# Half of an output projection done inside the last head's chunk loop, half a tile at a time

## The reference

```python
y = jnp.concatenate([y_hy, y_ml, y_rg], axis=-1)      # (2048, 1024)
x = x + gate2 * (y @ w_out)                            # output projection and residual
h = rmsnorm(x, norm2_g) * (1 + scale) + shift          # second norm
x = x + gate5 * (jnp.square(jax.nn.relu(h @ w1)) @ w2) # MLP, width 4096
out = rmsnorm(x, final_g)
```

## Time and profile before

| what | value |
|---|---|
| median of 3 runs | 2757.82 us |
| the profiled execution, its own time | 2759.13 us |
| its span in the profile | 2757.3 us |
| PE busy | 2550.4 us, 92% of the span |
| DVE busy | 1710.4 us, 62% |
| ACT busy | 1009.5 us, 37% |
| POOL busy | 456.4 us, 17% |

### The profile page before, as it was taken

One profiled execution on the slowest core, in us unless ns is written; L12 is line 12 of the kernel. 1 busy time (PEld: TensorE's weight loads), 2 busy tenths in 40 slices (PEclk: granted clock), 3 DMA queues, 4 the chain that ended last, 5 costly groups with the idle time before them and its releaser, 6 DMA issues.

```text
span 2757.3 us, 37657 instructions
## 1 busy us (share of the span) xinstructions
PE 2550.4 (92%) x14948; PEld 1394.5 (51%) x14948; DVE 1710.4 (62%) x2843; ACT 1009.5 (37%) x1960; POOL 456.4 (17%) x357
## 2 busy tenths in 40 slices
PE   6788999997779897996998999999999999999998
PEld 2445656543575876864454444444444444444443
DVE  5751545877975565648347877878776444544445
ACT  2744444457342332324455423333233321222122
POOL 0400003700105526104223111011110000000000
PEclk8899999998989898999999999999999999999999
DMA  7311112200102122013331534343347222122212
GB/s 211 101 51 42 35 43 73 74 27 1 27 9 71 55 33 62 26 40 83 71 130 65 186 104 145 117 143 118 131 141 245 79 84 84 43 84 84 84 58 62
DMA packets 138424, 229.12 MB, mean 83 GB/s; under 512 B 15080, under 2 KB 76008, under 8 KB 133640
## 3 DMA queue, kind: packets, MB, share of 16 engines
q1 hardware_dynamic: 136520, 220.41, 24.7%
q0 software_dynamic: 1728, 6.29, 0.7%
HBM read 163.60 MB, written 62.92 MB: 82 GB/s over the span
## 4 chain that ended last, share of the span: by engine, by line
PE 51%; DVE 2%; POOL 1%; issue 1%; ACT 0%; DVEq 0%; POOLq 0%; ACTq 0%
PE pb L2343 24%; PE pb L2283 21%; PE pb L2263 6%; POOL arena L1345 1%; PE pb L2252 1%; POOL MS L1337 0%; DVE arena L1808 0%; DVE arena L1816 0%; DVE arena L1887 0%; DVE arena L1769 0%; DVE arena L1898 0%; DVE arena L1637 0%; DVE arena L1873 0%; DVE arena L1765 0%; ACT arena L1200 0%
## 5 line engine op out<-in xcount | busy, mean ns | idle before, releaser
L2343 PE MATMUL pb<-arena 128*128 128x512 f16 x3072 | 667.9, 379 | 0.0
L2283 PE MATMUL pb<-arena 128*128 128x512 f16 (+2 forms) x2736 | 590.1, 377 | 8.8 <-DVE arena L1816 4.9
L2343 PEld LDWEIGHTS pb<-arena 128*128 128x128 f16 x3072 | 300.6, 98 | 362.4
L1898 DVE SCALAR_TENSOR_TENSOR arena<-pb,arena 128x512 f32<-128x512 f32 x512 | 352.4, 690 | 185.6 <-PE pb L2343 184.2
L307 PE MATMUL pb<-arena 128*128 128x512 f16 (+1 forms) x1992 | 424.2, 374 | 18.5 <-ACT arena L1086 7.7
L2283 PEld LDWEIGHTS pb<-arena 128*128 128x128 f16 x2736 | 267.3, 99 | 326.4 <-DVE arena L1816 6.1
L307 PEld LDWEIGHTS pb<-arena 128*128 128x128 f16 x1992 | 195.6, 99 | 245.5 <-issue 20.8
L1873 DVE TENSOR_TENSOR arena<-arena,pb 128x512 f32<-128x512 f32 x224 | 149.1, 683 | 251.2 <-PE pb L2283 251.2
L1229 ACT ACTIVATE arena<-arena 128x512 f32<-128x512 f32 x256 | 160.3, 626 | 172.2 <-DVE arena L1873 167.9
L1229 ACT ACTIVATE arena<-pb 128x512 f32<-128x512 f32 x32 | 19.0, 595 | 511.2 <-PE pb L2283 510.4
L1808 DVE SCALAR_TENSOR_TENSOR arena<-arena 128x512 f16<-128x512 f32 (+1 forms) x144 | 172.5, 1217 | 13.7 <-ACT arena L1177 13.4
(11 more groups left out here) (307 smaller groups left out, 3199.1 us busy)
## 6 DMA issues: line engine op xcount, KB each, us to landing
w1x<-arena SPq DMA_DIRECT2D x16, 1792.0 KB, 8.6
arena<-w1x SPq DMA_DIRECT2D x16, 1792.0 KB, 9.3
arena<-in_x SPq DMA_DIRECT2D x128, 128.0 KB, 4.1
arena<-in_mlp_w SPq DMA_DIRECT2D x64, 256.0 KB, 3.7
arena<-in_mlp_w SPq DMA_DIRECT2D x16, 1024.0 KB, 6.3
w2x<-arena SPq DMA_DIRECT2D x16, 1024.0 KB, 8.4
arena<-w2x SPq DMA_DIRECT2D x16, 1024.0 KB, 4.9
arena<-in_w_in SPq DMA_DIRECT2D x26, 512.0 KB, 4.0
```

Of the source, the lines that this page charges most:

```text
L1898: dve.scalar_tensor_tensor(xs, pb[:, 4 + n % 4, :], 1.0 / (WS * AS), xs, ALU.mult, ALU.add).then_inc(S("acc"), 1)
L2283: mm = pe.matmul(pb[:, (7 * g + j) % 4, c], W1P[g % 2][WDEST[a]][0][:, ws, P * k:P * k + P], token_op(b, L // 2, c)[:, k, hs, :], start=(k ...
L2343: mm = pe.matmul(pb[:, 4 + n % 4, :], ACTP[sl][:, 2 * f + th, hs, P * tt:P * tt + P], W2P[sl][:, f, ws, BLK * dh:BLK * dh + BLK], start=(f ...
```

## The change

- Eight of the 16 tiles of the output projection move into the last head's chunk loop: 16 halves, one at the end of each PE turn n = 4 to 15, two in n = 16 and 17, all into PSUM bank 1. DVE adds each to the residual at the end of its own turn of the same n.
- The output weights are made ready earlier: staged by column half, six gate products of POOL before the first chunk, two more after each of the first five YO; two `wo_hi` per ACT turn for n = 0 to 7 and two `wo_lo` per DVE turn for n = 1 to 8.
- ACT squares a whole finished tile in the loop (`loop_square`).
- SP loads x for six tiles right behind the first four w_out pieces, for two more later in the loop, and for the last eight after the loop.
- The output stage has eight steps s = 0 to 7. A step projects tile 8+s and transposes tiles 2s and 2s+1. Half of each affine (4 of 8 instructions) goes from ACT to DVE (`affine_hi`). POOL does its four `o_add` of a pair in one go, behind one power.

The core of the diff:

```diff
+        NEAR = (0, 1, 2, 3, 4, 6)
+        LATE = (5, 7)
+        LOOP_MM = {n: [(n - 4, 0)] if n < 8 else [(n - 8, 1)] for n in range(4, 12)}
+        LOOP_MM.update({12: [(4, 0)], 13: [(4, 1)], 14: [(5, 0)], 15: [(5, 1)], 16: [(6, 0), (6, 1)], 17: [(7, 0), (7, 1)]})
...
@@ SP
-            for i in range(EARLY):
-                load_tokens(sp, x1(i), ORD[i], S("x_in3"))
+            for g in range(4):
+                load_wo(g)
+            for i in NEAR:
+                load_tokens(sp, x1(i), ORD[i], S("x_in3"))
+            for g in range(4, 8):
+                sp.wait_ge(S("wo_lo"), 2 * (g - 3))
+                load_wo(g)
             sp.wait_ge(S("wo_lo"), 2 * KT)
+            for i in LATE:
+                load_tokens(sp, x1(i), ORD[i], S("x_in2"))
             sp.wait_ge(S("m_ylo"), NT * NH)
-            for i in range(EARLY, NT):
+            for i in range(HALF, NT):
                 load_tokens(sp, x1(i), ORD[i], S("x_in2"))
...
@@ ACT, turn n of the loop
-                    if h == NH - 1 and n >= 3:
-                        wo_hi(n - 3)
+                    if h == NH - 1 and n < 8:
+                        for i in (2 * n, 2 * n + 1):
+                            wo_hi(i)
+                    if h == NH - 1:
+                        for m in LOOP_SQ.get(n, ()):
+                            loop_square(m)
...
@@ POOL
+                if cn == NT * (NH - 1):
+                    for i in range(6):
+                        wo_gate(i)
...
+                if 0 <= c < 5:
                     pool.wait_ge(S("m_yo"), cn + 1)
+                    for i in (6 + 2 * c, 7 + 2 * c):
+                        wo_gate(i)
...
+            for s in range(1, HALF + 1):
+                t = HALF + s - 1
                 pool.wait_ge(S("h_ms"), N5 + t + 1)
                 pool.tensor_tensor(rst2[:, t:t + 1], ssq2[:, t:t + 1], mhalf[:], ALU.pow).then_inc(S("h_rs"), 1)
+                o_add(s - 1, (1, 2, 3, 4))
...
@@ DVE, turn n of the loop
-                    if h == NH - 1 and n >= 4:
-                        wo_lo(n - 4)
+                    if h == NH - 1 and 1 <= n < 9:
+                        for i in (2 * n - 2, 2 * n - 1):
+                            wo_lo(i)
...
+                    if h == NH - 1:
+                        for e, (m, dh) in enumerate(LOOP_MM.get(n, ())):
+                            if n == 4:
+                                dve.wait_ge(S("x_in3"), TOK0 + 16 * CPT * len(NEAR))
+                            if (m, dh) == (6, 0):
+                                dve.wait_ge(S("x_in2"), TOK0 + 16 * CPT * len(LATE))
+                            residual(home(m), dh, 1, loop_count(n, e + 1))
...
@@ DVE, output stage
+            for s in range(HALF):
+                t = HALF + s
+                normed(2 * s)
+                if s == HALF - 2:
+                    mean(t - 1)
+                if s < HALF - 1:
+                    normed(2 * s + 1)
+                if s >= 1:
+                    for i in (1, 2, 3):
+                        o_lo(s - 1, i)
+                if s == 0:
+                    dve.wait_ge(S("x_in2"), TOK0 + 16 * CPT * (len(LATE) + HALF))
+                residual(t, 0, 2 * (t % 2), 2 * t + 1)
+                if 1 <= s < HALF - 2:
+                    mean(t - 1)
+                affine_hi(2 * s)
+                if s < HALF - 1:
+                    affine_hi(2 * s + 1)
+                if s >= 1:
+                    for i in (4, 5, 6, 7):
+                        o_lo(s - 1, i)
+                if s == HALF - 1:
+                    w_add(0, (1, 2, 3))
+                    for i in (1, 2):
+                        w_lo(0, i)
+                residual(t, 1, 2 * (t % 2) + 1, 2 * t + 2)
...
@@ PE
+                def out_half(m, dh, count):
+                    pe.wait_ge(S("wo_lo"), KT * (dh + 1))
+                    pe.wait_ge(S("m_ylo"), NT * (NH - 1) + m + 1)
+                    if count >= 2:
+                        pe.wait_ge(S("o_x1"), count - 1)
+                    for k in range(KT):
...
                     if n >= 2:
                         ytr(n - 2)
+                    if h == NH - 1:
+                        for e, (m, dh) in enumerate(LOOP_MM.get(n, ())):
+                            out_half(m, dh, loop_count(n, e + 1))
...
-            for t in range(NT):
-                c0 = P * ORD[t]
+            for t in range(HALF, NT):
+                c0, s = P * ORD[t], t - HALF
...
-                    if dh == 0 and t >= 1:
-                        token_transposes(t - 1)
+                    if dh == 0:
+                        token_transposes(2 * s)
+                        if s < HALF - 1:
+                            token_transposes(2 * s + 1)
```

More of the change, by code:

```diff
@@ L1071, in wo_hi, with loop_square @@
             def wo_hi(i):
[L1072 removed]
+                k, c, src = wo_piece(i)
                 act.wait_ge(S("wo_m"), i + 1)
[L1074 removed]
+                act.activation(wop[:, k, 0, c], src, ACT.Copy, scale=WS).then_inc(S("wo_hi"), 1)
+            def loop_square(m):
+                done = LOOP_DONE[m]
+                act.wait_ge(S("o_x1"), done)
+                if m:
+                    act.wait_ge(S("h_sq"), N5 + m)
+                act.activation(junk_loop, x1(home(m)), ACT.Square, scale=1.0 / 32,
+                               accum_out=ssq2[:, home(m):home(m) + 1]).then_inc(S("h_sq"), 1)
             for h in range(NH):
@@ L1216, in _ @@
                 square(t, 1).then_inc(S("h_sq"), 1)
-                if t >= 2 and t % 2 == 0:
-                    for i in range(1, 6):
-                        o_hi((t - 2) // 2, i)
             for i in (3, 4, 5, 6):
@@ L1634, in wo_lo, with residual @@
             def wo_lo(i):
-                k, c = wo_half(i)
+                k, c, src = wo_piece(i)
                 dve.wait_ge(S("wo_hi"), i + 1)
-                dve.scalar_tensor_tensor(wop[:, k, 1, c], wos[k % 4][:, c], WS, wop[:, k, 0, c], ALU.mult, ALU.subtract
+                dve.scalar_tensor_tensor(wop[:, k, 1, c], src, WS, wop[:, k, 0, c], ALU.mult, ALU.subtract
                                          ).then_inc(S("wo_lo"), 1)
+            def residual(t, dh, bank, count):
+                c = slice(BLK * dh, BLK * dh + BLK)
+                dve.wait_ge(S("o_mm"), count)
+                dve.scalar_tensor_tensor(x1(t)[:, c], pb[:, bank, :], 1 / WS, x1(t)[:, c], ALU.mult, ALU.add
+                                         ).then_inc(S("o_x1"), 1)
             for h in range(NH):
@@ L1840, in _, with normed @@
                                          ).then_inc(S("h_ms"), 1)
-                dve.wait_ge(S("h_rs"), N5 + t + 1)
-                if t >= 2:
-                    dve.wait_ge(S("h_tr"), N5 + t - 1)
-                dve.tensor_scalar(xn2[t % 2], xt, rst2[:, t:t + 1], None, ALU.mult).then_inc(S("h_xn"), 1)
-                if t >= 2 and t % 2 == 0:
-                    for i in range(1, 4):
-                        o_lo((t - 2) // 2, i)
+            def normed(u):
+                dve.wait_ge(S("h_rs"), N5 + max(u + 1, HALF))
+                if u >= 2:
+                    dve.wait_ge(S("h_tr"), N5 + u - 1)
+                dve.tensor_scalar(xn2[u % 2], x1(u), rst2[:, u:u + 1], None, ALU.mult).then_inc(S("h_xn"), 1)
@@ new lines, in affine_hi @@
+            def affine_hi(u):
+                dve.wait_ge(S("h_tr"), N5 + u + 1)
+                if u >= 4:
+                    dve.wait_ge(S("s_lo"), 7 * (u // 2 - 1))
+                    dve.wait_ge(S("s_add"), 4 * (u // 2 - 1))
+                for k in range(KT // 2, KT):
+                    ins = dve.tensor_scalar(hf2[u % 4][:, k, :], pb[:, 5 + 2 * (u % 2), P * (k - 4):P * (k - 4) + P],
+                                            affA[:, 2, k:k + 1], affB[:, 2, k:k + 1], ALU.mult, ALU.add)
+                ins.then_inc(S("h_aff_hi"), 1)
@@ L1848, in _ @@
+            mean(NT - 1)
+            normed(NT - 1)
             for i in (3, 4, 5, 6):
                 w_lo(0, i)
+            affine_hi(NT - 1)
             for i in range(1, 8):
@@ L2219, in ytr @@
                     pe.transpose(pb[:, 0, 0:P], YO, ident[:]).then_inc(S("m_yt"), 1)
+                def out_half(m, dh, count):
[4 more added lines that the diff above has]
+                    for k in range(KT):
+                        for i, (ys, ws) in enumerate(((0, 0), (0, 1), (1, 0))):
+                            mm = pe.matmul(pb[:, 1, :], yT[:, k, ys, P * m:P * m + P], wop[:, k, ws, BLK * dh:BLK * dh + BLK],
+                                           start=(k == 0 and i == 0), stop=(k == KT - 1 and i == 2))
+                    mm.then_inc(S("o_mm"), 1)
                 for n in range(NT + 2):
```

113 lines of the change are left out of this document (53 added, 60 removed).

## The result

The changed kernel takes 2802.51 us (median of 4, 2793.29 to 2805.32), the one before 2757.28 beside it: a ratio of 1.0158, 95% interval 1.0134 to 1.0183, or +45.2 us. The forecast was slower by 26.4 and a range up to 2800. The direction was right; the size lies outside the range.

What follows compares the result with a forecast made beforehand. DVE bounds the loop (35.64 of 37.39 us), PE the output stage (180.52 of 180.55). Net +13.0, stage waits +11.4 and tail +2 gave +26.4 us on the median of 2757.82: 2784.2; range 2767 to 2800.

Steps and rivals of the forecast that it cites:

- the loop: Last head's loop: turns 1 to 3 +3.6, 4 to 15 +75.5 and -1.2, 16 and 17 +19.7; together +97.6 us.
- the wait for x: Output stage: the last eight x tiles load only after the loop, so PE waits 5.2 us before tile 2.
- the last steps over POOL: Output stage: steps of 12.9 us through POOL's additions against PE's 12.1, and 0.9 more where tile 13 must be finished.
- the tail: MLP start: weight additions and low parts stand ahead of the last residual while PE has nothing to do, about +2 us.
- eight tiles and a warm start given back: Output stage: eight tiles fewer save 82.9 us, and PE no longer starts at a low clock, 1.8: together -84.6.
- waits in the stage, to the end of the last half: Output stage: 5.2 us waiting for x plus 6.2 behind POOL's additions, together +11.4.
- A serial loop: Loop: DVE's next turn can't start during PE's half, 6.29 us per half; with waits behind it, chance 0.68.
- Rival 2: Loop: the half tiles fill PE's 24.9 idle us, so the kernel gets 21 us faster, 2736; chance 0.05.
- Rival 3: Loop: PE's clock falls; first half alone slow +1.8 us, all sixteen at 1.2 GHz +83, 2867; chance 0.06.
- the rule which the forecast weighed and charged nothing for: Output stage: DVE and POOL shut each other out, holding POOL up 1.0 us in each of 7 steps, +7.
- MLP weights: MLP start: weights land at about 1502, DVE wants them near 1508; hidden, with 6 us to spare.

Runs made afterwards that it cites:

- e2_late: Changed kernel with DVE adding each loop half to the residual one turn later, ahead of the forward state: 2757.5 us, ratio 0.9999.
- e10_fill: Changed kernel with 66 unused matmuls in PE's empty stretches of turns 15 to 17: 2802.1 us, ratio 1.0155.
- e3_xtile: Changed kernel with DVE waiting in the output stage for x of the one tile it needs, not all eight: 2789.2 us, ratio 1.0112.
- e5_hold: Changed kernel with loop residuals a turn later, and the last eight x loads held until the loop's 16th residual: 2763.4 us, ratio 1.0020.
- e7_tail: Changed kernel with the last residual added as soon as its half is done, ahead of low parts 4 to 7: 2802.1 us, ratio 1.0154.
- e4_warm: Changed kernel with unused matmuls in three PE waits: before transposing tiles 2 and 14, and before the MLP's first products: 2798.2 us, ratio 1.0150.
- e6_steps: Changed kernel with tile 14's second residual, mean and square ahead of tile 13's low and high parts in step 6: 2798.3 us, ratio 1.0141.
- e11_bestwarm: Changed kernel with later loop residuals, early halves in turns 7 to 12, earlier tile 14 mean and last residual, 50 unused matmuls before the MLP: 2748.9 us, ratio 0.9975.
- e12_best_again: Changed kernel with later loop residuals, early halves in turns 7 to 12, earlier tile 14 mean and last residual, run again: 2753.8 us, ratio 0.9984.

## Why the prediction was right, and where it failed

The direction and the mechanism were right: a loop in which DVE and PE take turns, and new waits behind it. What failed was the size of four terms: the loop (+5.0), the wait for x (+2.2), the last steps over POOL (+3.4) and the tail (+3.7). Together they are the 14.3 us between +26.4 and +40.7.

From the mark, in us; "measured" is the changed kernel's trace against the one before:

| term | forecast | measured |
|---|---|---|
| output stage entered | +97.6 | +102.6 |
| eight tiles and a warm start given back | -84.6 | -84.6 (taken as forecast) |
| waits in the stage, to the end of the last half | +11.4 | +17.0 |
| tail | +2 | +5.7 |
| sum | +26.4 | +40.7 |

The last half ends about 288.9 from the mark (1514.2), 253.9 before (1485.7): +35.0; less 102.6 - 84.6 = 18.0 that is 17.0. The two lower rows come from these ends, so they share whatever error they have. PE's own rows make up nearly all of the 17.0: waits of 7.05, 1.17 and 3.72, and 4.7 more at the low clock behind the first and the last. The warm start came as forecast: the stage's first half takes 5.35.

- **A serial loop: right.** "Nothing of DVE's next turn can start while PE does the half": turns of 9.45 and 10.64, waits of 5.60. e2_late shows the mechanism from the other side: with one DVE instruction in another place, the stage is entered 33.6 us earlier. Rival 2's mechanism (the holes fill) is then what happens, and only then; even so it brings the time only back to that of the kernel before.
- **Step that failed, the loop (+97.6 forecast, +102.6 measured):** the forecast took 5.18 for all sixteen halves, all at full clock. Rival 3 had the low clock as a case of its own, not as a part of the forecast, and looked at the longest hole of a plain turn. The granted clock was 1.00 in all plain turns and fell where the heads' work ends, in turns 15 and 16 (0.89 over 1355 to 1385); DVE's waits were 7.29 and 7.36 there, 3.4 more. e10_fill shows the empty stretch as the cause for turn 16, and makes it likely for turn 15. The other 1.6 are small pieces: the last YO ahead of turn 15's half is 72.5 later than before, where the forecast's terms give 71.6, and turns 16 and 17 take 0.7 more, 0.5 of it because the second half of a pair lands 6.21 behind the first and not 5.96. Rival 3's other case, the first half alone slow (+1.8), was not met in this trace; in e3_xtile, e5_hold and e7_tail it was (first residual some 2 us later).
- **The clock in the plain turns: right.** It was granted in full with PE 77% busy, against rival 3. The Trainium skill, "TensorE: Matmul & The Clock Gate", Part 1 on the clock gate, says that the throttled state is the default and activity releases it. The trace agrees for these turns (1.00), as the forecast had it.
- **Step that failed, the x wait (5.2, and 2.2 in the step behind it):** the 7.4 measured 9.2 (e3_xtile) to 9.9 (e5_hold). x landed 195.8 from the mark, where the forecast had 189.8 and the loop's 5.0 come on top: 1.0 late. But the eight `affine_hi` behind it took 2.63, not 1.6: 0.33 each, near the 0.35 that the forecast had as its other case, and not 0.20. And PE lost another 2.9 at the low clock, which e4_warm shows to be hidden behind POOL's chain, so it is no part of the price.
- **Step that failed, POOL's last steps (+4.0 forecast in the rest of the stage, 17.0 - 9.6 = 7.4 measured):** the step was 12.47 (12.9 forecast), and POOL's chain did set it, from tile 8's power to tile 12's. Its excess over PE's 12.1 cost PE nothing there, as PE was behind: the forecast's 0.8 in each of four steps did not come. The loss came in the last steps. Tile 13's power came 9.8 behind the one before, as its mean stands earlier; the next two took 15.2 and 17.2, and PE stood 1.17 and 3.72. For the 3.72 the forecast had no term: tile 14's mean stands behind the low parts that wait for POOL's fourth addition, and e6_steps, which moves it, leaves 1.03. The chain shows what else made these steps long: POOL's fourth addition (1494.66) waits for two `o_lo` that take 3.44 us beside POOL's own additions; three take 4.03 there and 1.90 in e3_xtile at 1420.22, beside none. That is the rule which the forecast weighed and charged nothing for, and the mechanism it left out: DVE and POOL hold each other up. The Trainium skill, "SBUF — State Buffer", section "Who interferes with whom", says that a DVE instruction with two SBUF inputs contends with a GpSimd one that reads SBUF. These rows agree (4.03 against 1.90). They have two full tiles as inputs; the scaling that the forecast took as its evidence (1.75 against 0.75) has one and a column of factors. The price in these two steps, about 2 each, is read from the rows; no run took it away alone.
- **Step that failed, the tail (+2 forecast, +5.7 measured):** the work ahead of the first `w_lo` and of the last residual was named, but only 2 us were charged for it. PE waited 4.61 for that first low part (L1870), and its 24 products behind the wait took 6.29 instead of 4.06, which had no term; the residual came 5.3 behind its half (1519.49). e7_tail, e4_warm and e11_bestwarm together show two limits of nearly the same length, that residual and the slow products: either fix alone won nothing. Both together were run only on top of the late residual, not on the changed kernel itself.
- **MLP weights: hidden, as forecast.** The first `w_add` starts at 1516.05 without a wait for them. Not so the store ahead of them: ACT waited 1.12 us for `b_extra` (3072 KB, landed 9.0 us behind its issue), and 2.9 to 3.0 in two other runs. The forecast's step on SP's queue looked at the loads and not at who waits for the store.

What stays open: why the first half tile of the loop, and the half of turn 15, is slow in some executions and not in others; what the holding up of DVE and POOL costs by itself; and where the 4.5 us lie that the medians show beyond the traces.

## What to carry to other kernels

Work put into an engine's idle time fits only if that time lies where the work's inputs are ready and its consumer isn't the next instruction of the engine that paces the loop: with a whole turn of slack for the consumer the same matmuls cost 34 us less here. When work is moved out of a stage, ask what it covered (here the loads of x, 9 to 10 us), and take the order of the semaphores that start those loads along. When two fixes each win nothing, look whether each hides the other before dropping them.

## What the runs showed of the hardware that was not expected

- Behind an empty stretch of 4.6 us, 24 matmuls of 384 columns took 6.29 us instead of 4.06; behind 7.05 us, 16 transposes 3.67 instead of 1.91. The granted clock over 1420 to 1430, with PE 44% busy, was 0.56 of full (2.4 GHz), near its lower level of 1.2.
- In turn 15 the half took 7.03 us behind empty stretches of 1.58 and 1.22 us with a little work between, and 5.34 behind the same stretches in e3_xtile and e7_tail; the same 1.58 in every turn before left the clock at 1.00.
- Unused matmuls in a wait keep the clock up (4.06 for the same 24 products), and gain time only where PE's next work is what is waited for.
- The store of `b_extra` (3072 KB) took 9.1 us from issue until ACT went on (1474.50 to 1483.62) in the changed kernel, and 11.0 in e4_warm (1474.68 to 1485.70).
- DVE and POOL hold each other up either way round, with the same instructions in the same order. In e12_best_again three `o_lo` took 5.10 us and POOL's addition beside them 1.62; in e11_bestwarm, which differs only behind them, the `o_lo` took 1.89 and the addition 3.43. Which of the two was held up changed from one execution to the other.
